# The first layer's gated recurrence: heads in step, or each head one chunk behind the last

## The reference, cut to what matters

```python
    scores = jnp.einsum('nbhid,nbhjd->nbhij', q_dec, k_inv) * causal
    o_intra = jnp.einsum('nbhij,nbhjv->nbhiv', scores, v)

    def step(state, xs):
        q_c, k_c, v_c, decay = xs
        o_c = jnp.einsum('bhid,bhdv->bhiv', q_c, state)
        state = state * decay[..., None] + jnp.einsum('bhjd,bhjv->bhdv', k_c, v_c)
        return state, o_c
```

## Time and profile before

| | us |
|---|---|
| median of the runs (lowest, highest) | 1195.35 (1194.51, 1198.39) |
| the profiled execution's own time | 1193.62 |
| its span in the trace | 1191.7 |
| TensorE busy | 1154.0 (97%) |
| VectorE busy | 891.9 (75%) |
| ScalarE busy | 742.0 (62%) |

### The profile page before, as it was taken

How to read it: one execution, slowest core, us unless ns; L and a number is a source line. 1 busy time by engine, 2 the same in 40 slices (tenths; PEclk the granted TensorE clock), 3 DMA queues, 4 the chain that set the end, 5 groups by cost and what they waited for, 6 DMA issues and landing times.

```text
span 1191.7 us, 16868 instructions
## 1 busy us (share of the span) xinstructions
PE 1154.0 (97%) x5780; PEld 927.0 (78%) x5780; DVE 891.9 (75%) x1168; ACT 742.0 (62%) x910; POOL 137.2 (12%) x100
## 2 busy tenths in 40 slices
PE   5999999999999999999999999999999999999996
PEld 4778888786788888888778885686788888888775
DVE  6642346735899999999886548836899999999875
ACT  5553220234788788888746439734788788788654
POOL 0000000000121221221100000001022122121100
PEclk9999999999999999999999999999999999999998
DMA  9482211142699999999682220243799999999631
GB/s 380 183 310 106 71 36 64 43 177 106 228 353 392 376 373 389 370 381 389 242 350 90 76 102 1 72 141 112 250 354 393 376 376 385 375 379 389 252 138 70
DMA packets 50085, 287.58 MB, mean 241 GB/s; under 512 B 9216, under 2 KB 9216, under 8 KB 20721
## 3 DMA queue, kind: packets, MB, share of 16 engines
q1 hardware_dynamic: 34256, 243.06, 53.9%
q0 software_dynamic: 15776, 43.82, 9.9%
HBM read 272.68 MB, written 30.41 MB: 254 GB/s over the span
## 4 chain that ended last, share of the span: by engine, by line
PE 85%; DVE 7%; ACT 3%; DMA 3%; issue 2%; SPq 0%; POOLq 0%; DVEq 0%; ACTq 0%
PE psum L479 80%; PE psum L789 2%; DVE arena L2331 2%; ACT whi L1183 1%; DMA arena<-vscr,cur 1%; DVE arena L2344 1%; PE psum L830 1%; DMA raw<-w_dense_dram 1%; PE psum L546 1%; ACT ahi L1183 1%; DVE wlo L1703 1%; PE psum L710 1%; DVE alo L1759 0%; DMA arena<-yscr 0%; DMA yscr<-arena,cur 0%
## 5 line engine op out<-in xcount | busy, mean ns | idle before, releaser
L1703 DVE TENSOR_TENSOR wlo<-raw,whi 128x2048 fp32r<-128x2048 f32 x213 | 485.9, 2290 | 95.0 <-ACT whi L1183 85.8
L479 PE MATMUL psum<-whi,ahi 128*128 128x512 f32 (+1 forms) x1184 | 471.1, 398 | 10.1 <-issue 3.4
L479 PE MATMUL psum<-wlo,ahi 128*128 128x512 f32 (+1 forms) x1184 | 459.0, 388 | 0.0
L479 PE MATMUL psum<-whi,alo 128*128 128x512 f32 (+1 forms) x1184 | 458.0, 388 | 0.0
L1183 ACT ACTIVATE whi<-raw 128x2048 fp32r<-128x2048 f32 (+1 forms) x215 | 409.7, 1907 | 76.7 <-PE psum L479 73.9
L479 PEld LDWEIGHTS psum<-whi,ahi 128*128 128x128 f32 x1184 | 223.4, 189 | 57.6 <-issue 6.9
L479 PEld LDWEIGHTS psum<-whi,alo 128*128 128x128 f32 x1184 | 223.1, 188 | 46.5
L479 PEld LDWEIGHTS psum<-wlo,ahi 128*128 128x128 f32 x1184 | 223.8, 189 | 40.7
L1183 ACT ACTIVATE arena<-psum 128x512 f32<-128x512 f32 (+1 forms) x141 | 80.9, 584 | 133.2 <-PE psum L479 105.1
L1183 ACT ACTIVATE ahi<-psum 128x512 fp32r<-128x512 f32 x146 | 81.8, 593 | 89.0 <-PE psum L789 39.0
L479 PE MATMUL psum<-arena 128*128 128x512 f32 (+9 forms) x802 | 122.2, 323 | 0.2
(11 more groups left out here) (194 smaller groups left out, 866.2 us busy)
## 6 DMA issues: line engine op xcount, KB each, us to landing
raw<-w_moe_dram SPq DMA_DIRECT2D x192, 1024.0 KB, 9.0
raw<-w_dense_dram SPq DMA_DIRECT2D x35, 1024.0 KB, 7.7
yscr<-arena POOLq DMA_DIRECT2D x2, 4096.0 KB, 23.2
arena<-yscr POOLq DMA_DIRECT2D x8, 1024.0 KB, 7.0
vscr<-arena POOLq DMA_DIRECT2D x8, 512.0 KB, 2.9
arena<-w_proj_dram POOLq DMA_DIRECT2D x2, 1024.0 KB, 6.8
arena<-gains_dram POOLq DMA_DIRECT2D x3, 512.0 KB, 3.9
out_dram<-arena SPq DMA_DIRECT2D x3, 512.0 KB, 2.6
```

The costliest lines, as they stand in the source:

```text
L479: return nc.tensor.matmul(o, l, r, start=start, stop=stop, **kw)
L1703: tt(wlo[:, b % SPL, :], raw[:, b % RAW, :], halves(whi[:, b % SPL, :]), ALU.subtract).then_inc(lo_ready, 1)
```

## The change

The four heads are staggered: at step r, head hh works on chunk r - hh. There are STEPS_A = 19 steps, r = 0 to 18.

* Scores of block tb move into projection g, after its piece (1, tb), each block into a bank of its own (4 to 7). DVE masks them all between splits(9) and splits(10), into AR_F, in place of the transposed k (K^T), which is no longer needed. The area ST is gone.
* A step has up to four parts on TensorE: updates of heads 0 and 1 (banks 4 and 5), the in-chunk product of head r mod 4, the reads of all heads (four different chunks mod 4, so four column groups), updates of heads 2 and 3 (banks 4 and 5 again, other columns), these behind a wait for the first round's count `g_U`. The two updates of a round lie on different 32-row groups and in different banks.
* TensorE waits for the state of step r-1 (`g_S`) at the top of the step, ahead of the updates. DVE's updates of the state stay 60, with up to four for each step, each with its own block and decay column.
* Head outputs of block tb go to bank 7 or 6 in turn. `intra` of block tb waits for ACT's copy of block tb-2. ACT's copy waits for step 4 tb + 6.
* DVE's squares come at step 4t + 7, the rest of the norm at 4t + 9; before at 5t + 5 and 5t + 7.

```diff
@@ -314,6 +314,29 @@
         def nhalf(tb, half):
             return (ORDER[3] * 2 + half) * TB + tb + 1
+        STEPS_A = NCH + HEADS - 1
+        def heads_U(r):
+            return [hh for hh in range(HEADS) if 0 <= r - hh < NCH - 1]
+        def rounds_U(r):
+            pairs = [[hh for hh in heads_U(r) if hh // 2 == j] for j in range(2)]
+            return [p for p in pairs if p]
+        def done_U(r):
+            return sum(len(rounds_U(j)) for j in range(r + 1))
+        def U_bank(hh):
+            return PS[4 + hh % 2][:, hh * P:(hh + 1) * P]
+        def out_bank(tb):
+            return PS[7 - tb % 2]
         def first_key(n):
@@ -602,68 +625,71 @@
             dense(BLK["q"], "act", after=lambda i, q: cum(q) if i == 1 else None)
             dense(BLK["v"], "act", after=lambda i, q: kq_T(q) if i == 1 else None)
-            dense(BLK["g"], "act")
             KT_, QT_ = area(AR_F, TB, 512), area(AR_Q, TB, 512)
             Kt, V = area(AR_K, TB, 512), area(AR_V, TB, 512)
-            S, ST = area(AR_S, HEADS, P), area(AR_ST, HEADS, P)
+            S, ST = area(AR_S, HEADS, P), area(AR_F, TB, 512)
             def scores(tb):
                 if tb == 0:
                     pe.wait_ge(g_KT, TB)
                     pe.wait_ge(g_QT, TB)
+                for hh in range(HEADS):
+                    last = mm(PS[4 + tb][:, hh * P:(hh + 1) * P], KT_[:, tb, hh * P:(hh + 1) * P],
+                              QT_[:, tb, hh * P:(hh + 1) * P], True, True)
+                last.then_inc(g_sc, 1)
+            dense(BLK["g"], "act", after=lambda i, q: scores(q) if i == 1 else None)
+            def update(r, hh):
+                tb, c = (r - hh) // CPB, (r - hh) % CPB
+                rows = slice(c * CHUNK, (c + 1) * CHUNK)
+                return mm(U_bank(hh), Kt[rows, tb, hh * P:(hh + 1) * P],
+                          V[rows, tb, hh * P:(hh + 1) * P], True, True)
+            def intra(tb, hh):
+                if hh == 0 and tb >= 2:
+                    pe.wait_ge(g_o, tb - 1)
+                return mm(out_bank(tb)[:, hh * P:(hh + 1) * P], ST[:, tb, hh * P:(hh + 1) * P],
+                          V[:, tb, hh * P:(hh + 1) * P], hh == 0, False, skip_group_check=True)
+            def inter(n, hh):
+                tb, c = n // CPB, n % CPB
+                rows = slice(c * CHUNK, (c + 1) * CHUNK)
+                return mm(out_bank(tb)[rows, hh * P:(hh + 1) * P],
+                          QT_[:, tb, hh * P + c * CHUNK:hh * P + (c + 1) * CHUNK],
+                          S[:, hh, :], False, c == CPB - 1 and hh == HEADS - 1,
+                          skip_group_check=True)
+            def rec(r):
+                if r >= STEPS_A:
+                    return
+                if r == 0:
                     pe.wait_ge(g_v, TB)
                     pe.wait_ge(g_ktail, TB)
-                else:
-                    pe.wait_ge(g_scm, tb)
+                    pe.wait_ge(g_scm, TB)
+                pe.wait_ge(g_S, r + 1)
+                rounds = rounds_U(r)
+                if rounds:
+                    for hh in rounds[0]:
+                        last = update(r, hh)
+                    last.then_inc(g_U, 1)
+                hh = r % CPB
+                if r - hh < NCH:
+                    last = intra((r - hh) // CPB, hh)
                 for hh in range(HEADS):
-                    last = mm(PS[4][:, hh * P:(hh + 1) * P], KT_[:, tb, hh * P:(hh + 1) * P],
-                              QT_[:, tb, hh * P:(hh + 1) * P], True, True)
-                last.then_inc(g_sc, 1)
-            def intra(tb):
-                pe.wait_ge(g_scm, tb + 1)
-                if tb > 0:
-                    pe.wait_ge(g_o, tb)
-                for hh in range(HEADS):
-                    mm(PS[7][:, hh * P:(hh + 1) * P], ST[:, hh, :],
-                       V[:, tb, hh * P:(hh + 1) * P], hh == 0, False, skip_group_check=True)
-            def chunk(n):
-                tb, c = n // CPB, n % CPB
-                rows = slice(c * CHUNK, (c + 1) * CHUNK)
-                if n >= 2:
-                    pe.wait_ge(g_S, n)
-                if n < NCH - 1:
-                    for hh in range(HEADS):
-                        last = mm(PS[5 + n % 2][:, hh * P:(hh + 1) * P],
-                                  Kt[rows, tb, hh * P:(hh + 1) * P],
-                                  V[rows, tb, hh * P:(hh + 1) * P], True, True)
+                    if 0 < r - hh < NCH:
+                        last = inter(r - hh, hh)
+                last.then_inc(g_in, 1)
+                if len(rounds) > 1:
+                    pe.wait_ge(g_U, done_U(r) - 1)
+                    for hh in rounds[1]:
+                        last = update(r, hh)
                     last.then_inc(g_U, 1)
-                if n > 0:
-                    pe.wait_ge(g_S, n + 1)
-                for hh in range(HEADS):
-                    last = mm(PS[7][rows, hh * P:(hh + 1) * P],
-                              QT_[:, tb, hh * P + c * CHUNK:hh * P + (c + 1) * CHUNK],
-                              S[:, hh, :], False, c == CPB - 1 and hh == HEADS - 1,
-                              skip_group_check=True)
-                last.then_inc(g_in, 1)
-            def rec(s):
-                tb, r = s // 5, s % 5
-                if tb >= TB:
-                    return
-                if r == 0:
-                    scores(tb)
-                    return
-                if r == 1:
-                    intra(tb)
-                chunk(tb * CPB + r - 1)
             pe.wait_ge(g_S, 1)
             for b, name in enumerate("CHB"):
@@ -1336,8 +1362,10 @@
             def out_rows(tb):
-                act.wait_ge(g_in, CPB * (tb + 1))
-                copy(K[:, tb, :], PS[7][:, :]).then_inc(g_o, 1)
+                r = CPB * tb + CPB + HEADS - 2
+                act.wait_ge(g_in, r + 1)
+                act.wait_ge(g_U, done_U(r))
+                copy(K[:, tb, :], out_bank(tb)[:, :]).then_inc(g_o, 1)
             def out_root(tb):
                 act.wait_ge(g_osum, tb + 1)
@@ -1814,7 +1842,7 @@
                 dve.wait_ge(g_esf, tb + 1)
                 tt(K[:, tb, :], K[:, tb, :], yt, ALU.mult).then_inc(g_ktail, 1)
             splits(6)
-            S, ST = area(AR_S, HEADS, P), area(AR_ST, HEADS, P)
+            S = area(AR_S, HEADS, P)
             nc.vector.memset(S, 0.0).then_inc(g_S, 1)
             for tb in range(TB):
                 dve.wait_ge(g_silu, tb + 1)
@@ -1829,31 +1857,23 @@
             def rec(s):
-                tb, r = s // 5, s % 5
-                if tb < TB and r == 0:
-                    dve.wait_ge(g_sc, tb + 1)
-                    if tb > 0:
-                        dve.wait_ge(g_in, CPB * (tb - 1) + 1)
-                    tt(ST, PS[4][:, :].rearrange("p (a b) -> p a b", a=HEADS),
-                       hc("triI").unsqueeze(1).to_broadcast([P, HEADS, P]), ALU.mult)\
-                        .then_inc(g_scm, 1)
-                n = tb * CPB + r - 1
-                if tb < TB and r > 0 and n < NCH - 1:
-                    dve.wait_ge(g_U, n + 1)
-                    dve.wait_ge(g_in, n + 1)
-                    for hh in range(HEADS):
-                        last = stt(S[:, hh, :], S[:, hh, :], dec[:, tb, hh, n % CPB:n % CPB + 1],
-                                   PS[5 + n % 2][:, hh * P:(hh + 1) * P], ALU.mult, ALU.add)
+                if heads_U(s):
+                    dve.wait_ge(g_U, done_U(s))
+                    dve.wait_ge(g_in, s + 1)
+                    for hh in heads_U(s):
+                        tb, c = (s - hh) // CPB, (s - hh) % CPB
+                        last = stt(S[:, hh, :], S[:, hh, :], dec[:, tb, hh, c:c + 1],
+                                   U_bank(hh), ALU.mult, ALU.add)
                     last.then_inc(g_S, 1)
-                t = (s - 5) // 5
-                if s >= 5 and s % 5 == 0:
+                t = (s - 7) // 4
+                if s >= 7 and s % 4 == 3 and t < TB:
                     dve.wait_ge(g_o, t + 1)
                     dve.wait_ge(g_sc, t + 1)
                     link(tt(F[:, t, :], K[:, t, :], K[:, t, :], ALU.mult))
                     nc.vector.tensor_reduce(ssb[:, t, 0:4],
                                             F[:, t, :].rearrange("p (a b) -> p a b", a=HEADS),
                                             AX, ALU.add).then_inc(g_osum, 1)
-                if s >= 5 and s % 5 == 2:
+                if s >= 9 and s % 4 == 1 and t < TB:
                     dve.wait_ge(g_oroot, t + 1)
                     dve.wait_ge(g_g, TB)
                     link(nc.vector.reciprocal(ssb[:, t, 4:8], ssb[:, t, 4:8]))
@@ -1891,6 +1911,12 @@
             splits(8)
             splits(9)
+            for tb in range(TB):
+                dve.wait_ge(g_sc, tb + 1)
+                tt(F[:, tb, :].rearrange("p (a b) -> p a b", a=HEADS),
+                   PS[4 + tb][:, :].rearrange("p (a b) -> p a b", a=HEADS),
+                   hc("triI").unsqueeze(1).to_broadcast([P, HEADS, P]), ALU.mult)\
```

(5 more changed lines are left out.)

## The result

The changed kernel takes 1186.24 us (four runs, 1183.63 to 1186.72) against 1196.1 for the kernel before (the three runs from the start and one more): ratio 0.9915, 95% interval 0.9895 to 0.9934. That is 9.9 us, where 5.6 were forecast and 1189.7 expected. The profiled executions differ by less than the medians: 1193.62 against 1186.45 us, 7.2 apart (spans 1191.7 and 1184.6). Two questions follow: why 7.2 and not 5.6, and why the medians have some 3 us more.

The account below looks back on a forecast made before the run. TensorE, busy 97% of the span, was taken as the bound; its 8.2 us balance less stalls of 1.9 and 0.7 gave 5.6 saved, 1193.62 to 1188.0, and with 1.7 for the median 1189.7 us, range 1186.1 to 1194.0.

Parts of the forecast that it names:

- the bound: From projection g to the convolution's last gate, TensorE alone limits: a microsecond off it is one off the kernel.
- the overlap: In a full recurrence step, paired updates take 0.43 us and four reads at once 0.35, at 0.11 per slot; step 1.63.
- My slots from the attention's pairs: Layer 1's attention: eight records one after another 1.08 us, in pairs 0.65, so 0.11 us per slot, applied to the recurrence.
- rival B: Reads of the state stay one after another, 0.65 us more per full step, 9.3 in all; 1197.9 us, chance 0.04.
- Rivals A: Reads overlap only two column groups at a time, 0.22 us more in each of 14 steps; 1192.4 us, chance 0.07.
- mode changes: Switching TensorE between dense and tiled products costs 5.4 us after against 4.2 before, so 1.2 us lost.
- the move: The four score products go into projection g but get no cheaper, 3.2 us.
- TensorE's own balance: Recurrence parts save 9.4 us, less 1.2 for changes between dense and tiled products: 8.2 us gained.
- the stall at step 9: TensorE waits 1.9 us for the state: chain of sum, root, high and low part takes 9.5 us against 7.6.
- the table load counts: ScalarE's 1.28 us table load for block 0's root stands behind the wait for the sum, so inside the chain.
- the second stall: TensorE waits 0.7 us for the state at step 17, chunk 14's chain taking 7.4 us against 6.8, without table load.
- Rival D: New waits ahead of updates or second round drain TensorE 0.3 us in each of 14 steps, 4.2; 1193.9 us, chance 0.11.

## Why the prediction was right and wrong

*Right: the bound.* TensorE's one piece of the chain was the limit, and the stretch shrank by what TensorE saved less the stalls. The gate came at 222.23 where I had about 224.

*Right: the overlap.* The full step of 1.63 us is 1.61, with two updates and four reads at once. My slots from the attention's pairs carried over from 64 to 32 and from two groups to four: a group of reads for 1, 2, 3 and 4 heads takes 0.336, 0.343, 0.350 and 0.356 us, so each further column group costs 7 ns. The Trainium skill ("TensorE: Matmul & The Clock Gate", Part 3: Packing small matmuls) has about 4 ns for a further tile; this trace has 7. Its sentence that LDWEIGHTS overlaps matmuls in flight only when the row group differs, on which rival B stood, does not hold here: four weight loads of 128 rows and different column groups start within 0.02 us of 154.21, while the first read's matmul, which starts at 154.21 too, is in flight. Rivals A and B are out by the same rows.

*Right: mode changes and the move.* The move of the scores changed the stretch by nothing, and TensorE's own balance was 8.6 us (7.47 in the stretch and 1.12 of stalls) where I had 8.2. The nineteen steps take 26.3 us (forecast 26.6) and the changes of mode cost 1.2, as I had it. Two blemishes of the sum: 18 x 0.27 + 4 x 0.10 + 0.25 is 5.5 and not 5.4, and the 0.42 for the in-chunk product stands without its working; it measured 0.42.

*Wrong: the stall at step 9*, the term "the table load counts". I had 1.9 us, the trace has 0.52. I read the idle time of one table load at 112.66 as a rule that a load stands behind its instruction's wait. The root's own load at 158.39 could not tell, since its sum was long there. The activation at 112.66 has two waits (for the normed rows and for projection g), the root at step 9 has one. With two, the load stands behind the later one; with one, it runs ahead of it. The load ran while ScalarE idled anyway. With a second wait added it moved into the chain, and the stall became 1.87 us. That is 1.35 us of the 1.9 between forecast and trace in the stretch (5.6 and 7.5); TensorE's balance and the second stall make up the rest. The chain itself was right: at step 17, without a load, 0.7 were forecast and 0.60 came, and with ScalarE's list turned both stalls went.

*Rival D* did not occur: no gap stands ahead of the second round.

*Wrong: nothing gained outside the stretch*, the step that took the end to be the same "from the gate at 229.46 on" and carried the sum over to the median. Even without either stall that sum gives 8.2 us, and the averages are 10.6 apart. Outside the stretch 3 us were gained that no term of mine held: 0.7 in the scatter between the layers, some 0.3 more at that boundary in the traces, where fewer traces of staggered kernels have a piece at half clock, and the rest in timed runs only, with its cause open. My sum was made on one profiled execution, 1193.62 us, which has a mean clock of 0.996 and lies 2.2 us below the average of 54 runs. I took its distance from the median, 1.7 us, as common to both kernels. The changed kernel has no such distance (1186.45 profiled, 1185.3 on average). What lowers it is only partly shown.

## What to carry to other kernels

Where small products share an array with dense ones on a busy TensorE, count groups of row or column tiles, not products: here one more fp32 product run at once cost 7 ns, the same product in sequence 0.21 us (two records), and a full-array product between tiled ones 0.22 us a step more than next to the dense ones. So put it next to them. When a step of a chain gets shorter, recompute for each step what its state waits for on the slower engines, and move weight splits ahead of waits for results. An instruction inserted ahead of another, as a table load is, may or may not be behind its wait: before reading its place off another row, see that the same number of waits stands there.

## What the runs showed of the hardware

A stall can cost more than its length. In the kernel with two waits TensorE idled 1.8 us ahead of 168.41, and from 169.5 its clock was granted at 1.2 GHz for 3.4 us, the only such piece inside the recurrence in all eighteen traces. A stall need not do it: ahead of step 4 of the kernel with the scores moved TensorE idled 1.18 us, and the clock stayed at 2.4 GHz. Busy time and clock before, in and after it (columns as above):

```profile
166.00:169.50 3.50, 1.71 (x17) 0.94 (x15) 2.35 (x5) 0.00 (x0) 0.00 (x0) 1.00 0.33 70
169.60:173.00 3.40, 3.40 (x14) 2.66 (x11) 2.48 (x7) 0.00 (x0) 0.00 (x0) 0.51 0.54 227
173.10:176.50 3.40, 3.40 (x27) 2.26 (x26) 0.97 (x4) 0.21 (x1) 0.00 (x0) 1.00 0.00 0
```

Step 9 took 1.92 us in place of 1.61, and the dense piece behind it 4.17 in place of 2.96, so 1.5 us more were lost behind a stall of 1.87. With the 1.35 by which the stall grew this accounts for the 2.8 us by which the stretch of that kernel (125.90) is longer than the changed kernel's.
